# State space stage: the products of decays with x taken in pairs, broadcasts and weight steps moved around them

## The reference, cut to what matters

```python
CB = jnp.einsum('bclgn,bcsgn->bcgls', Cc, Bc)
Lmat = segsum_exp(a)                      # exp of differences of running sums, lower triangle
y_diag = jnp.einsum('bcgls,bgrcls,bcsgrp->bclgrp', CB, Lmat, X)
...
y = (y_diag + y_off).reshape(Bsz, S, SSD_HEADS, P) + D_skip[:, None] * x_heads
y = y.reshape(Bsz, S, SSD_D_INNER) * jax.nn.silu(z)
y = rmsnorm_2(y.reshape(Bsz, S, G, SSD_D_INNER // G), norm_g)
```

## Time and profile before

| what | value |
|---|---|
| median of 3 runs | 963.61 us (963.34 to 963.86) |
| profiled execution | 963.97 us |
| its span | 962.0 us |
| PE busy | 953.4 us (99%) |
| DVE / ACT busy | 634.6 / 520.2 us |
| mean granted TensorE clock | 0.999 of full speed |
| stage of the change | about 481.8 to 540 us |

### The profile page before, as it was taken

How to read it: one execution, slowest core, us unless ns; L and a number is a source line. 1 busy time by engine, 2 the same in 40 slices (tenths; PEclk the granted TensorE clock), 3 DMA queues, 4 the chain that set the end, 5 groups by cost and what they waited for, 6 DMA issues and landing times.

```text
span 962.0 us, 16219 instructions
## 1 busy us (share of the span) xinstructions
PE 953.4 (99%) x6674; PEld 861.6 (90%) x6674; DVE 634.6 (66%) x824; ACT 520.2 (54%) x790; POOL 62.7 (7%) x113
## 2 busy tenths in 40 slices
PE   9999999999999999999999999999999999999997
PEld 7877889989988888989977999998998899999996
DVE  5778685777555555778857787776666466555554
ACT  5577554555444444566865674545555445444443
POOL 3100001001000000314000001100000010000001
PEclk9999999999999999999999999999999999999999
DMA  9974436456655656556464455455655346665661
GB/s 306 313 238 129 146 88 177 157 173 206 199 187 178 194 177 197 154 179 194 141 193 136 129 174 199 157 189 165 202 164 172 113 154 219 184 202 170 196 190 45
DMA packets 133545, 170.39 MB, mean 177 GB/s; under 512 B 5824, under 2 KB 97296, under 8 KB 133472
## 3 DMA queue, kind: packets, MB, share of 16 engines
q1 hardware_dynamic: 131408, 165.07, 54.3%
q10 hardware_dynamic: 1424, 2.84, 0.9%
q0 software_dynamic: 640, 1.44, 0.6%
HBM read 168.28 MB, written 1.05 MB: 176 GB/s over the span
## 4 chain that ended last, share of the span: by engine, by line
PE 90%; DVE 5%; ACT 2%; issue 1%; DMA 1%; POOL 0%; POOLq 0%; DVEq 0%; ACTq 0%
PE ps L374 13%; PE ps L375 13%; PE ps L376 13%; PE ps L405 8%; PE ps L406 8%; PE ps L407 8%; PE ps L740 5%; PE ps L739 5%; PE ps L738 5%; PE ps L357 4%; PE ps L461 3%; DVE parts L1564 2%; DVE room L1598 1%; PE ps L492 1%; PE ps L493 1%
## 5 line engine op out<-in xcount | busy, mean ns | idle before, releaser
L1564 DVE TENSOR_TENSOR parts<-raws,parts 128x1024 fp32r<-128x1024 f32 (+2 forms) x307 | 367.5, 1213 | 220.2 <-ACT parts L1041 219.7
L1041 ACT ACTIVATE parts<-raws 128x1024 fp32r<-128x1024 f32 (+2 forms) x307 | 315.7, 1045 | 233.7 <-PE ps L376 131.5
L374 PE MATMUL ps<-room_r,parts 128*128 128x256 f32 x1248 | 351.9, 282 | 0.1
L375 PE MATMUL ps<-room_r,parts 128*128 128x256 f32 x1248 | 348.9, 280 | 0.0
L376 PE MATMUL ps<-room_r,parts 128*128 128x256 f32 x1248 | 348.4, 279 | 0.0
L374 PEld LDWEIGHTS ps<-room_r,parts 128*128 128x128 f32 x1248 | 234.6, 188 | 6.1 <-issue 4.3
L375 PEld LDWEIGHTS ps<-room_r,parts 128*128 128x128 f32 x1248 | 234.6, 188 | 1.3
L376 PEld LDWEIGHTS ps<-room_r,parts 128*128 128x128 f32 x1248 | 234.7, 188 | 0.0
L405 PE MATMUL ps<-parts,room_r 128*128 128x512 f32 (+1 forms) x336 | 134.4, 400 | 1.3 <-DVE parts L1564 1.3
L407 PE MATMUL ps<-parts,room_r 128*128 128x512 f32 (+1 forms) x336 | 131.1, 390 | 0.0
L406 PE MATMUL ps<-parts,room_r 128*128 128x512 f32 (+1 forms) x336 | 131.1, 390 | 0.0
(11 more groups left out here) (226 smaller groups left out, 877.3 us busy)
## 6 DMA issues: line engine op xcount, KB each, us to landing
raws<-in_w_in SPq DMA_DIRECT2D x99, 512.0 KB, 4.5
raws<-in_w_ffn_in SPq DMA_DIRECT2D x44, 512.0 KB, 4.0
raws<-in_w_up SPq DMA_DIRECT2D x32, 512.0 KB, 4.4
raws<-in_w_down SPq DMA_DIRECT2D x32, 512.0 KB, 4.1
raws<-in_w_ffn_out SPq DMA_DIRECT2D x22, 512.0 KB, 4.1
raws<-in_w_xkv SPq DMA_DIRECT2D x16, 512.0 KB, 3.7
raws<-in_w_out SPq DMA_DIRECT2D x8, 512.0 KB, 4.2
raws<-in_w_up_ssd SPq DMA_DIRECT2D x8, 512.0 KB, 5.1
```

The source lines that it names most:

```text
L374: e.matmul(ps, wh, hT[0][:, k, :], start=k == 0, stop=False)
L375: e.matmul(ps, wh, hT[1][:, k, :], start=False, stop=False)
L1041: e.activation(t.h, t.raw, ACT.Copy).then_inc(s["hi"], 1)
L1564: e.tensor_tensor(t.l, t.raw, t.h.bitcast(F32), ALU.subtract).then_inc(s["lo"], 1)
```

## The change

`diags` is unchanged: (0,0), (0,1), (1,0), (1,1), (0,2), (0,3), (1,2), (1,3). Now `diag` i and `diag` i + 1 (i even) stand directly behind each other, with steps before and after the pair. The number of steps is the same, 21.

```diff
             step(3)
             for i, (t, q) in enumerate(diags):
-                if i in (1, 3):
-                    seg((i + 3) // 2)
-                step()
+                if i % 2 == 0:
+                    step(2)
+                if i in (0, 2):
+                    seg(i // 2 + 2)
+                if i == 6:
+                    y_out(1, 0)
+                diag(t, q)
+                if i % 2 and i < 6:
+                    step(2)
+                if i == 3:
+                    y_out(0, 0)
                 if i == 7:
                     y_out(0, 1)
-                diag(t, q)
-                if i < 6:
-                    step()
-                if i in (2, 4):
-                    y_out(i // 2 - 1, 0)
             step(3)
             y_out(1, 1)
             step()
```

## The result

The changed kernel takes 971.54 us (median of 5 runs, 971.37 to 972.35) against 963.61 us (5 runs, 963.34 to 963.87): a ratio of 1.0083, 95% interval 1.0072 to 1.0093. It is 7.9 us slower; 970.9 was forecast. The profiled execution has a span of 969.3 us, 7.3 more than before.

What follows compares the result with a forecast made beforehand. PE was taken to bound the kernel, busy for 953.4 of 962.0 us. Pairing -0.8, first wait +1.6, second wait +5.5 and clock +1.0 gave +7.3 us, a median of 970.9 us, range 968.4 to 973.2.

Steps and rivals of the forecast that it cites:

- The pairing saves 0.8 us: Eight lone diag groups become four pairs on PE, each saving 0.20 us of seams: -0.8 us, bounds 0 and -1.0.
- The first wait, +1.6, for a bank of `seg(3)` at step 13: PE at step 13 waits until ACT's later seg(3) empties its first bank: +1.6 us, between 1.1 and 1.8.
- `diag` 5 is next in line and covered: diag 5 needs E(0, 3) from DVE at T + 7.95; PE arrives at T + 8.4, otherwise waits 1.1 us.
- The second wait, +5.5: PE before y_out(0, 1), as DVE stands at y_T(1, 0) until step 17: +5.5 us, bounds 3.6 and 6.6.
- One aside of the prediction: Between the two transposes on PE there were before three steps, 8.4 us and more; now only two diags.
- Nothing after that: y_out(1, 1), three steps behind y_out(0, 1), is covered by 1.1 us; what follows only shifts.
- The signs: Expected in the profile: PE waits of 5.5 and 1.6 us, long DVE idle, paired diag rows, starts 0.43 to 0.47 apart.
- The clock, +1.0: After the long wait TensorE falls from 2.4 to 1.2 GHz for a while: +1.0 us, bounds 0 and 1.8.
- The start's 1.8: About 1.8 us lost at the kernel's start from rest, taken as the upper bound of the clock's cost.
- The sum: -0.8 + 1.6 + 5.5 + 1.0 = +7.3 us: profiled execution 963.97 to 971.3, median 963.61 to 970.9 us.

Runs made afterwards that it cites:

- the pairs alone: Changed kernel with y_out(0, 0) moved back to step 9 and y_out(1, 0) to step 14: 962.46 us against 963.60, ratio 0.9987.
- the run that keeps PE busy: Changed kernel with 20 products of the identity by itself (40 instructions) in the long wait before y_out(0, 1): 970.07 us, ratio 1.0067.
- 10 products: Changed kernel with 10 products of the identity (20 instructions) in the long wait before y_out(0, 1): 971.86 us, ratio 1.0086.
- 10 instructions: Changed kernel with 5 products of the identity in the long wait before y_out(0, 1): 971.83 us, ratio 1.0085.

## Why the prediction was right, point by point

- *The pairing saves 0.8 us:* right in kind, mis-sized. It saves 4 x 0.36 = 1.45 by the rows and 1.43 in the stage of the pairs alone, which is outside the bounds that the prediction gave (0 to -1.0). What it had wrong is the split of a lone group into 0.61 of its own and 0.20 of seams. The second group of a pair costs 1.26 - 0.81 = 0.45, 0.028 us for an instruction, so 0.16 of the 0.61 comes only once in a pair and is saved with the seam.
- *The first wait, +1.6, for a bank of `seg(3)` at step 13:* 1.64 idle, 1.87 by starts. Shown to be ACT's place in line: with ACT's `seg(3)` earlier, or with `y_out(0, 0)` back at step 9, it goes. That it is the first of the two banks rests on the time, 510.66 against 510.76, and on the queue followed.
- *`diag` 5 is next in line and covered:* right. Uncovered, it waits 1.2 us.
- *The second wait, +5.5:* 5.51 idle, 5.69 by starts. `y_out(1, 0)` to `y_out(0, 1)` took 8.25 us, the figure of the prediction. Shown from two sides: PE's order changed (964.20) and DVE's and ACT's order changed (965.31). One aside of the prediction is off: before the change four steps stood between the two transposes, not three, 13.3 us (513.20 to 526.49). No term rests on it.
- *Nothing after that:* right. In the changed kernel no wait is listed behind `y_out(0, 1)`.
- *The signs:* PE's long wait and the pace of 0.43 came as described. The first wait was to be released by ACT L1384; the view names nobody. A pair was to reach the next L405 in 1.2 us and takes 1.08 (513.72 to 514.80), the same mis-sizing as above. DVE was to have a long idle time that ends at the transposes; its idle times there are 1.6, 2.1 and 1.05 us, with a tile between each, since it goes on with tiles while it stands at `y_T(1, 0)`.
- *The clock, +1.0:* right in kind, mis-sized. The fall is shown, by the granted clock of 0.50 and by the run that keeps PE busy. Its price was taken too low: 1.57 in the profile. The start's 1.8 was the nearer row, and the half of it that I took had nothing behind it.
  The Trainium skill (TensorE: Matmul & The Clock Gate, section "Part 1: The HAM clock gate") says that a long gap brings the lower level back; this trace, with 0.50 behind a rest of 5.5 us, agrees.
- *The sum:* +7.3 was forecast for the profiled execution and +7.3 measured, with luck. Two errors, 0.65 too little saved by the pairs and 0.6 too little lost to the clock, cancel. A third, that each wait delays PE by more than its idle time (0.4 in all), is hidden by a profiled execution of the kernel before that lost 0.6 elsewhere. The medians differ by 7.9. Two of the five runs, 971.85 and 972.35, have a mean granted clock of 0.994 and 0.995 where the profiled one has 0.996, which fits a longer slow stretch in them; they have no profile.

## What to carry to other kernels

An order written out for several engines is one order: when a piece that hands work over moves later on one engine, look at what stands behind its receiver in the other engines' order, and who waits for that. Here no profile has a wait for the late transpose's own result, but DVE stood waiting for it, and the next piece in DVE's order was work that PE wanted 2.6 us later. Price such a wait by the same chain a few microseconds earlier in the trace, and follow a queue of banks by hand. Take the delay from start to start, since here the idle time listed for PE was less than what the wait cost. Where PE bounds the kernel and gets a wait of several microseconds, add the clock's price to it as a range.

## What the runs showed of the hardware

- Rests of PE of 1.05 us (20 products) and 1.64 us (changed kernel, step 13) were followed by full pace; rests of 3.28, 4.40 and 5.51 us by a granted clock of 0.50 (1.2 GHz) and starts of 512-column matmuls 0.43 us apart in place of 0.23.
- The slow stretch behind such a rest lasted from 3.4 us (534.23 to 537.63 with 10 products) to 5.9 us (534.16 to 540.05), and cost 1.5 to 2.6 us, 0.44 to 0.45 of its length. It did not follow the length of the rest.
- Twenty products of the identity, 40 instructions in 4.6 us, kept the clock up in the profile (1.00) and were worth 1.5 us by the medians; 20 and 10 instructions left rests of 3.28 and 4.40 us and won nothing.
- Going from a weight product of 128-column weights to a group with 64-column weights and back costs 0.36 us in all, which is 0.81 for a lone group of 16 instructions less the 0.45 of a second one directly behind. How the 0.36 divides between the seams and the group's own start, no run shows.
- A wait of PE delayed it by 0.2 us more than the idle time listed: 1.87 for 1.64 and 5.69 for 5.51.
